# Order of the loads and halvings around the context's output layer, buffers of x's modulation, and the heads' order

## What is computed

```python
mod_x = split(silu(c) @ ada_w[layer] + ada_b[layer], 6)        # 24 parts of 512 columns in all
mod_c = split(silu(c_ctx) @ ada_w[layer] + ada_b[layer], 6)
h_x = modulate(rmsnorm(x, g0), mod_x[0], mod_x[1])              # h * (1 + scale) + shift
h_c = modulate(rmsnorm(ctx, g0), mod_c[0], mod_c[1])
# layer 0: both streams
a = softmax(q1 k1) - lam_val * softmax(q2 k2)                   # 4 differential heads, then rmsnorm of each
b = softmax(q [k_neighbours; k_ctx] + bias)                     # 8 neighbourhood heads (ctx: plain)
x = x + mod_x[2] * (concat(a, b) @ w_out_ab)
ctx = ctx + mod_c[2] * (concat(a_c, b_c) @ w_out_ab)
x = x + mod_x[5] * swiglu(modulate(rmsnorm(x, g1), mod_x[3], mod_x[4]), w1, w3, w2)
ctx = ctx + mod_c[5] * swiglu(modulate(rmsnorm(ctx, g1), mod_c[3], mod_c[4]), w1, w3, w2)
# swiglu(h) = (silu(h @ w1) * (h @ w3)) @ w2, hidden width 2816
# layer 1: 16 query heads, window and sinks, w_out_c, the same swiglu, for x alone
```

## Time and profile before

| | |
|---|---|
| median of 3 executions | 3745.43 us (3737.53 to 3749.34) |
| profiled execution | 3745.17 us |
| span of the profile | 3743.4 us |
| TensorE busy (weight loads beside it) | 3386.2 us (3102.8) |
| VectorE, ScalarE busy | 2395.5 us, 1891.3 us |
| granted TensorE clock, mean | 0.943 |
| moved by DMA | 723.49 MB |

### The profile page before, as it was taken

How to read it: one execution, slowest core, us unless ns; L and a number is a source line. 1 busy time by engine, 2 the same in 40 slices (tenths; PEclk the granted TensorE clock), 3 DMA queues, 4 the chain that set the end, 5 groups by cost and what they waited for, 6 DMA issues and landing times.

```text
span 3743.4 us, 56592 instructions
## 1 busy us (share of the span) xinstructions
PE 3386.2 (90%) x24411; PEld 3102.8 (83%) x24411; DVE 2395.5 (64%) x3026; ACT 1891.3 (51%) x2229; POOL 0.2 (0%) x4
## 2 busy tenths in 40 slices
PE   7978989989689899999999998996788979998798
PEld 6968989988689799999999997873677878885598
DVE  6756655568566588888888887444553454454454
ACT  5454444444534477776777776223455443333443
POOL 0000000000000000000000000000000000000000
PEclk9989999999899899999999999896799989999899
DMA  6423455444234599899998996204122344421153
GB/s 235 167 89 111 164 210 192 167 162 157 81 123 160 217 366 358 328 359 338 338 356 332 353 352 242 105 35 191 68 88 113 138 191 169 176 84 68 47 190 113
DMA packets 102671, 723.49 MB, mean 193 GB/s; under 512 B 11664, under 2 KB 13328, under 8 KB 16528
## 3 DMA queue, kind: packets, MB, share of 16 engines
q1 hardware_dynamic: 102416, 719.80, 51.6%
HBM read 718.71 MB, written 1.05 MB: 192 GB/s over the span
## 4 chain that ended last, share of the span: by engine, by line
PE 76%; DVE 11%; ACT 8%; DMA 2%; issue 2%; SPq 0%; DVEq 0%; ACTq 0%
PE PS L1354 13%; PE PS L1355 13%; PE PS L1356 13%; PE PS L1307 6%; PE PS L1305 6%; PE PS L1306 6%; DVE WL L2053 3%; ACT WH L1673 3%; PE PS L1611 3%; PE PS L1609 3%; PE PS L1610 3%; PE PS L1421 2%; PE PS L1450 2%; PE PS L1384 1%; PE PS L1438 1%
## 5 line engine op out<-in xcount | busy, mean ns | idle before, releaser
L2053 DVE TENSOR_TENSOR WL<-RAW,WH 128x2048 fp32r<-128x2048 f32 (+3 forms) x428 | 963.1, 2252 | 670.7 <-ACT WH L1673 665.6
L1673 ACT ACTIVATE WH<-RAW 128x2048 fp32r<-128x2048 f32 (+3 forms) x428 | 803.1, 1878 | 292.0 <-PE PS L1356 174.4
L1354 PE MATMUL PS<-PH,WH 128*128 128x256 f32 x2464 | 717.3, 291 | 42.0 <-DVE PL L2219 12.3
L1355 PE MATMUL PS<-PL,WH 128*128 128x256 f32 x2464 | 702.8, 285 | 0.0
L1356 PE MATMUL PS<-PH,WL 128*128 128x256 f32 x2464 | 702.7, 285 | 0.0
L1354 PE MATMUL PS<-HPH,WH 128*128 128x256 f32 (+1 forms) x1648 | 502.6, 305 | 54.6 <-issue 18.4
L2053 DVE TENSOR_TENSOR WL<-F,WH 128x2048 fp32r<-128x2048 f32 x210 | 481.3, 2292 | 86.8 <-ACT WH L1673 85.8
L1354 PEld LDWEIGHTS PS<-PH,WH 128*128 128x128 f32 x2464 | 477.3, 194 | 50.7 <-issue 35.0
L1355 PE MATMUL PS<-HPL,WH 128*128 128x256 f32 (+1 forms) x1648 | 486.2, 295 | 0.0
L1356 PE MATMUL PS<-HPH,WL 128*128 128x256 f32 (+1 forms) x1648 | 485.7, 295 | 0.0
L1355 PEld LDWEIGHTS PS<-PL,WH 128*128 128x128 f32 x2464 | 477.6, 194 | 1.3
(11 more groups left out here) (379 smaller groups left out, 5286.3 us busy)
## 6 DMA issues: line engine op xcount, KB each, us to landing
F<-in_moe_w SPq DMA_DIRECT2D x210, 1024.0 KB, 5.8
RAW<-in_ffn_w SPq DMA_DIRECT2D x130, 1024.0 KB, 4.8
RAW<-in_moe_w SPq DMA_DIRECT2D x126, 1024.0 KB, 5.1
RAW<-in_w_in SPq DMA_DIRECT2D x64, 1024.0 KB, 4.8
RAW<-in_ada_w SPq DMA_DIRECT2D x22, 1024.0 KB, 4.8
F<-in_ada_w SPq DMA_DIRECT2D x18, 1024.0 KB, 10.9
RAW<-in_w_kv SPq DMA_DIRECT2D x16, 1024.0 KB, 4.8
RAW<-in_w_in_ab SPq DMA_DIRECT2D x12, 1024.0 KB, 5.4
```

The costliest lines, as they stand in the source:

```text
L1354: T_.matmul(out, lh, rh, start=first, stop=False)
L1355: T_.matmul(out, lh, rl, start=False, stop=False)
L1673: S.activation(mem["WH"][:, t.s % NHL, 0:m], v.raws[t.slot][:, 0:m], ACT.Copy).then_inc(*ac.done("w_hi", t.s))
L2053: V.tensor_tensor(mem["WL"][:, t.s % NHL, 0:m], v.raws[t.slot][:, 0:m], mem["WH"][:, t.s % NHL, 0:m].bitcast(F32), sub).then_inc(*dv.done( ...
```

## The change

Five things are different in the program.

1. `wab0`'s first two tiles are begun, and the first is asked to be halved (with one more ahead), in front of the context's heads; `put("tile", ("wab0", 0), 2)` behind the first three quarters of the heads is gone.
2. In `head`, x's differential and neighbourhood heads (`part` 1) are "roomy": the score products of both maps are put together, then both exponentials, then both normalisations, and the planner's pauses behind them are longer, so that transposes come later.
3. The w1 blocks of `g0c` have evac `silu_tanh`: ACT writes tanh(0.5 x), DVE (y + 1) * x from the accumulator bank in an operation of its own and frees the bank; `up` multiplies by 0.5 and by the w3 block. The other feed-forward layers keep `silu`.
4. Two buffers of their own, 16 (in `PQ`) and 17 (`G5`), for two pairs of modulation tiles, which used to go through the ring before the first and second group of `g0x`. The former third pair is no longer asked for in `g0x`.
5. `place_tiles` keeps a wait that a tile brings with it.

```diff
-        u = 0.43 * nk / 256
+        u, roomy = 0.43 * nk / 256, spec["kind"] in ("diff", "near") and spec["part"]
...
+            together = range(members) if roomy else None
             for qb in range(qbs):
-                for m in range(members):
-                    while len(self.banks.held) > 6:
-                        yield 0.3
-                    self.bank(("s", name, qb, m), self.bgc, True)
-                    self.put("s", name, qb, m, cost=2 * u if spec["kind"] == "mem" else u + 0.43 * bias)
-                    if qb == qbs - 1 and m == members - 1:
-                        self.scored.add(name)
-                    yield 1.5
-                    if m == 0:
-                        self.pp.take(("pp", name, qb), self.ppc, True)
-                    else:
-                        self.tmp.take(("tmp", name, qb, m), self.tmpc, True)
-                    self.small[name, qb, m] = 4 * (self.n["small"] % 32)
-                    self.n["small"] += 1
-                    self.put("e", name, qb, m)
-                    self.banks.let(("s", name, qb, m))
-                    yield 2.0
-                    self.put("n", name, qb, m)
-                    if m:
-                        self.tmp.let(("tmp", name, qb, m))
-                    yield 1.5
+                for some in [together] if roomy else [[m] for m in range(members)]:
+                    for m in some:
+                        while len(self.banks.held) > 6:
+                            yield 0.3
+                        self.bank(("s", name, qb, m), self.bgc, True)
+                        self.put("s", name, qb, m, cost=2 * u if spec["kind"] == "mem" else u + 0.43 * bias)
+                        if qb == qbs - 1 and m == members - 1:
+                            self.scored.add(name)
+                        yield 0.8 if roomy and m < members - 1 else 1.5
+                    for m in some:
+                        if m == 0:
+                            self.pp.take(("pp", name, qb), self.ppc, True)
+                        else:
+                            self.tmp.take(("tmp", name, qb, m), self.tmpc, True)
+                        self.small[name, qb, m] = 4 * (self.n["small"] % 32)
+                        self.n["small"] += 1
+                        self.put("e", name, qb, m)
+                        self.banks.let(("s", name, qb, m))
+                        yield 1.2 if roomy and m < members - 1 else 2.5 if roomy else 2.0
+                    for m in some:
+                        self.put("n", name, qb, m)
+                        if m:
+                            self.tmp.let(("tmp", name, qb, m))
+                        yield 0.8 if roomy and m < members - 1 else 3.5 if roomy else 1.5
                 self.bank(("t", name, qb), self.bgc)
                 self.put("t", name, qb, cost=u)
                 self.pp.let(("pp", name, qb))
...
-            t.after = [("p_hi", "mg1", 7), ("lo", "mg1", 3), ("ps", "br2_1", 7)]
+            t.after = t.after or [("p_hi", "mg1", 7), ("lo", "mg1", 3), ("ps", "br2_1", 7)]
...
-        s1 = Stage(f"{name}a{i}", "rows", "silu", w1, 8, g * 128, nfb * 128, src, n=n, **ready)
+        s1 = Stage(f"{name}a{i}", "rows", gate_by, w1, 8, g * 128, nfb * 128, src, n=n, **ready)
...
     p.lin_all(av)
+    wab0 = Stage("wab0", "rows", "res", io["w_out_ab"], 8, 0, D, "HP", norm="ab0", gate=(0, 0, 1))
+    p.begin(wab0, 0)
+    p.begin(wab0, 1)
+    p.put("tile", ("wab0", 0), 1)
     p.soon(True)
     for i in range(4):
         p.head(f"d0.{i}", 256, members=2, sub=True, kind="diff", part=0, i=i)
     p.halves("ab0", (4, 5, 6, 7, 0, 1, 2, 3), lambda i: [f"n0.{2 * i - 8}", f"n0.{2 * i - 7}"] if i > 3 else [f"d0.{i}"])
...
-    p.put("tile", ("wab0", 0), 2)
...
-    p.lin_all(Stage("wab0", "rows", "res", io["w_out_ab"], 8, 0, D, "HP", norm="ab0", gate=(0, 0, 1)), p.follow("c0.1"))
+    p.lin_all(wab0, p.follow("c0.1"))
...
-                 hooks={"end": heads_done}, after=p.follow("c1.0"), gate=(0, 1, 1))
+                 hooks={"end": heads_done}, gate_by="silu_tanh", after=p.follow("c1.0"), gate=(0, 1, 1))
...
-    def one_pair():
-        p.modulation(1, [0, 1])
-        p.modulate()
+    p.modulation(1, [16, 17], [("lo", "ab1", 3), ("lo", "c1.0", 3)])
+    p.modulation(1, [16, 17])
     p.norm("x1.0", src="X", tmp="G4v", gn=(1, 0, 0), dst="HP", n0=0, of="g0xc2")
-    swiglu_order(p, "g0x", io["ffn_w1_2"][0], io["ffn_w3_2"][0], "ffn_w2_2_0", 2816, "HP", ("HD0", "HD1"), dict(norm="x0.1"), "res", hooks={i: one_pair for i in range(3)},
+    swiglu_order(p, "g0x", io["ffn_w1_2"][0], io["ffn_w3_2"][0], "ffn_w2_2_0", 2816, "HP", ("HD0", "HD1"), dict(norm="x0.1"), "res", hooks={i: p.modulate for i in range(3)},
                  after=p.follow("x1.0"), gate=(0, 1, 0))
...
+    v.raws += [mem["PQ"][:, 0:2048], G[5].rearrange("p a n -> p (a n)")]
...
+        elif kind == "silu_tanh":
+            ac.wait_ge("ps", name, i)
+            ac.freed(plan.tmp.before["tmp", name, i])
+            S.activation(tmp(("tmp", name, i), g.n), ps, ACT.Tanh, scale=0.5).then_inc(*ac.done("tanh", name, i))
...
+            elif kind == "silu_tanh":
+                y = tmp(("tmp", name, i), g.n)
+                dv.wait_ge("tanh", name, i)
+                V.scalar_tensor_tensor(y, y, 1.0, ps, add, mult).then_inc(*dv.done("free_d", name, i))
             elif kind == "up":
                 y, hid = tmp(("tmp", g.more["other"], i), g.n), v.pair[g.more["hid"]]
-                dv.wait_ge("free_a", g.more["other"], i)
                 dv.wait_ge("ps", name, i)
-                V.tensor_tensor(y, y, ps, mult).then_inc(*dv.done("free_d", name, i))
+                if plan.stage[g.more["other"]].evac == "silu":
+                    dv.wait_ge("free_a", g.more["other"], i)
+                    V.tensor_tensor(y, y, ps, mult).then_inc(*dv.done("free_d", name, i))
+                else:
+                    dv.wait_ge("free_d", g.more["other"], i)
+                    V.scalar_tensor_tensor(y, y, 0.5, ps, mult, mult).then_inc(*dv.done("free_d", name, i))
                 dv.wait_ge("hid_hi", name, i)
```

More of the change, by code:

```diff
@@ L308, in block @@
             self.bank((g.name, i), None, side == 0)
-            if g.evac in ("conv_ml", "silu", "gate"):
+            if g.evac in ("conv_ml", "silu", "silu_tanh", "gate"):
                 self.tmp.take(("tmp", g.name, i), self.tmpg)
@@ L832, in ml_chain, with swiglu_order @@
     p.ml_done.add(hd)
-def swiglu_order(p, name, w1, w3, w2, f, src, hids, ready, evac, n=T, hooks={}, after=None, **more):
+def swiglu_order(p, name, w1, w3, w2, f, src, hids, ready, evac, n=T, hooks={}, after=None, gate_by="silu", **more):
     fb = f // 128
```

## The result

The changed kernel takes **3690.6 us** (median of 4, 3684.98 to 3697.84) against 3745.56 (median of 4): ratio 0.9857, interval 0.9832 to 0.9882, 1.4% faster. The forecast was 3698, its range 3671 to 3726. The profiled execution took 3684.98 us (span 3683.2), 60.2 us less than the one of before. Of these, 5.0 us lie ahead of the stage `av`, in code that has not changed; in the fourteen profiled executions of this study `av` began anywhere between 2486.5 and 2501.0 us.

A forecast was written before the change was run, and what follows sets the result against it. TensorE, busy 90% of the span, was taken as the bound, so time is won only where it stands still or runs at its lower clock. Terms summing to -47.5 us took 3745.2 to 3698 us, range 3671 to 3726.

The forecast's parts named there:

- head terms: Output layer's stage, first feed-forward part and local heads together: transposes wait less for softmax normalisation; 26 us saved, bounds 5 to 45.
- first feed-forward part: Four two-map heads of the context's feed-forward, to 2768.7: waits of 9.3 and 8.01 us partly go; -8, bounds nothing or 17.3.
- local heads: Eight heads, 2768.7 to 2949.9: later transposes cover much of 20.1 us of waits, some slow clock goes; -14.
- Early tiles: Before the output layer: its first two tiles loaded and halved ahead of the modulation remove PE's whole hole; -12.4 us.
- Output layer's stage: Heads in the new order there: the transposes' 3.74 us wait and a little slow clock go; -4 us.
- Silu as tanh: Context's feed-forward: 31 table loads fewer, 22 more DVE operations; taken as 0, bounds 0 and +10.6 us.
- Rival 2: ACT was the true brake, table load and Silu standing before the halving: 45 us gained in the heads, 3679; chance 0.20.
- rivals 1 and 4: Head stages: VectorE becomes the bound, 3724, chance 0.15; or DVE frees banks late and PE waits, 3781, chance 0.05.
- x's feed-forward: Second and third group of x's stage: holes before them go with modulation pairs moved; -11.6 and -13.1 us.
- First group: Start of x's feed-forward stage: its first tile is now third in SP's queue; +4.7 us, between 0 and 6.
- Tail: Before g1: leftover modulation pair delays the norm 3.6 us and g1's first tile 7.3 more; +10.9, between 7 and 13.

## Why the prediction was right, and where not

The forecast of -47.5 stands against -55.2 in the profiled execution from `av` on and -55 in the medians. The two loading parts came out by their mechanism. The head terms agree in their sum, -26 forecast and -26.7 measured, but part of that is luck: up to the end of the first feed-forward part -12 were forecast and -3.7 came, in the local heads -14 and -23.0. Some 4 us of each difference are the ten matmuls that changed their stage (an estimate from their durations in the trace after), the rest is not.

- *Early tiles*, -12.4: right, -13.9, and -11.7 when alone. The reason given (landing and both halvings ahead of the normalisation) fits the trace, and PE's idle time there fell by 11.4 (31.2 to 19.8); the shares of landing and halvings are not shown.
- *Output layer's stage*, -4: **wrong, +2.9**. The step said that the wait of 3.74 goes. It went, and so did the 8.01 at 2678.69, which also lies in this stage though the prediction booked it in the next. But the root-mean-square step of the first differential head now stands behind the norm: PE waits 5.80 us at 2668.56 for its square (L1837), which ACT computes behind the norm's high halves, and 4.64 us at 2631.61 for a square of the norm, which stands behind an exponential that waits 3.55 us for DVE's maximum. The two new waits and one of 1.24 for a normalisation make 11.7 us, as much as the two old ones (11.75); PE's idle time in the stage is 23.0 before and 23.1 after. The waits moved. The +2.9 itself is busy time, 47.6 to 50.4 us, with 14 matmuls more in the stage. With the early tiles left out, order and tanh gave 68.6 us here, -2.1, at clock 0.86 and idle time 21.2; four other traces with this stage's instructions as in the changed kernel took 72.4 to 77.1. So a loss is not shown either. The timeline after the change:

```profile
2630.47 0.69 ACT L1813 ACTIVATE TMP<-PS,SM 128x512 f32<-128x512 f32 x1 [3.55 <-DVE SM L2263]
...
2631.61 0.79 PE L1391 MATMUL PS<-G,CST 128*128 128x256 f32 x1 [4.64 <-ACT G L1699]
...
2668.56 0.80 PE L1465 MATMUL PS<-TMP,CST 128*128 128x256 f32 x1 [5.80 <-ACT TMP L1837]
```

- *First feed-forward part*, -8: -6.6, the number right. Its wait for a copy (L1910) stayed, 3.70 to 3.60. That it is a gain is not shown: without the new order for the differential heads this part took 6.1 us more, but the stages on either side 2.9 and 1.8 less.
- *Local heads*, -14: **mis-sized, -23.0**. Without the 4 us of the ten matmuls that left the stage it is still 5 more than forecast. The step counted half of the waits and little of the slow clock, and priced tanh at nothing. Measured on this stage: order alone 15.5, tanh on top of it 7.5. The expected new wait for the copies of the transposes came at 0.85 us, once, not at 1 to 2 for each pair.
- *Silu as tanh*, 0: **wrong**, see above. ACT was not the bound (busy 155 of 296 us in the head stages), but its table loads stood in front of halvings and exponentials on the way to the normalisation. Rival 2 had the mechanism, a part beside the order and not in its place; its size, 45 us for the three head terms, did not come (26.7).
- *DVE as the bound, banks freed late* (rivals 1 and 4): neither. DVE's busy time in the head stages rose from 146.7 to 149.5 us, and no wait of PE there is for a bank that DVE frees.
- *x's feed-forward*, -24.7: right, -27.0; both holes are gone and the first tiles take 5.7 us instead of 8.1.
- *First group*, +4.7: right, hole +4.83, stage +5.7.
- *Tail*, +10.9: the hole grew by 7.40 us where 7.3 was forecast, and `wc` to `g1` took 9.3 us more; 3.2 came back in `cq`, where the clock was 0.97 against 0.92. The same instructions ran there at 0.90 in two later runs, so no run shows this as an effect of the change.

## What to carry to other kernels

A wait in an in-order queue is paid by all that stands behind it: ask of each load what it waits for and which load behind it is due next; twice here a pair that nothing needed soon stood ahead of weights that PE waited for. When such a wait is removed, the next one in the same queue decides, and a planner may move work in front of it. In a stage with many short waits, count the matmuls at the lower clock with the holes: here they were half of the gain (13.4 of 26.7 us). And when a change moves work across the border of a stage, compare a stretch that holds the same instructions on both sides: the new order of the differential heads looked like a gain of 6 us in one stage, and over three stages none can be told.

## What was not expected of the hardware

The same instructions in the same stage ran at different clocks: `cq` took 79.9 us at granted clock 0.97, 83.1 at 0.92 and 84.8 at 0.90 in different executions, PE's idle time being 5.2 to 5.7 us in each. In the stage of the context's heads two executions of one list of instructions differed by 4.0 us, and `wab0` took 72.4 to 77.1 us in five executions with the same instructions, at clock 0.82 to 0.77, with 22.9 to 23.3 us of PE idle in each. A part worth under some 4 us in such a stage can't be read from one profile by its time; PE's idle time repeats far better.
